# Cutting a streaming encoder step into segments of 128, 256, 256, 256 and 128 + 64 tokens, with row streams that begin and end by themselves

## What is computed

```python
h = layer_norm(x)
P = h @ w_in                          # RWKV-7 columns and differential-attention columns
m = concat(rwkv7(P_rw), diff_attn(P_da)) @ w_out
h = layer_norm(alpha * h + m)
# PEER, for each token: 8 heads, each with 16 rows of two tables of 16384 x 1024
q = h @ wq;  s = q . subkeys          # 2 x 128 scores a head
idx, gate = best 16 of the sums of the best 16 + 16;  softmax
act = gelu(u_tab[idx] . h)            # 128 rows of 4 KB a token
y = layer_norm(alpha * h + sum(gate * act * v_tab[idx]))   # 128 rows more
```

## Time and profile before

| | us |
|---|---|
| median of three runs | 3923.53 |
| lowest and highest run | 3910.43, 3933.09 |
| span of the profiled execution | 4295.2 |
| TensorE busy in it | 2933.3 |
| VectorE busy | 2496.8 |
| GpSimd (POOL) busy | 2395.1 |
| ScalarE busy | 663.3 |
| HBM read | 1315.76 MB, 309 GB/s over the span |

### The profile page before, as it was taken

The page is one execution under the profiler, slowest core; times in us unless marked ns, Lnnn a source line. Parts: engine busy times, 40 slices in busy tenths (PEclk is TensorE's granted clock), DMA queues, the critical chain, the costliest instruction groups (busy, mean ns, idle before and its releaser), DMA issues.

```text
span 4295.2 us, 49152 instructions
## 1 busy us (share of the span) xinstructions
PE 2933.3 (68%) x18591; PEld 1591.0 (37%) x18591; DVE 2496.8 (58%) x5849; ACT 663.3 (15%) x1879; POOL 2395.1 (56%) x2194
## 2 busy tenths in 40 slices
PE   7886376777757777678567777677546565575677
PEld 5666354436324434345034343354112221230111
DVE  3437987665965555578755556569645455583311
ACT  3331122220012212101011222200011111000000
POOL 0001366664556665675665566565566667676765
PEclk9988677898878877789787887788776666687788
DMA  3125688898889987898987898898899889999998
GB/s 117 67 78 205 217 314 308 313 339 348 298 322 337 336 307 274 337 372 323 357 333 277 317 341 293 306 377 310 318 392 355 322 340 356 391 389 347 383 359 315
DMA packets 372965, 1330.61 MB, mean 310 GB/s; under 512 B 40348, under 2 KB 75576, under 8 KB 361592
## 3 DMA queue, kind: packets, MB, share of 16 engines
q0 software_dynamic: 314576, 1145.45, 71.2%
q1 hardware_dynamic: 58152, 182.02, 11.3%
HBM read 1315.76 MB, written 11.29 MB: 309 GB/s over the span
## 4 chain that ended last, share of the span: by engine, by line
PE 19%; issue 15%; DVE 13%; POOL 10%; another core or an unknown queue 8%; DMA 6%; ACT 2%; DVEq 0%; ACTq 0%
PE pacc L1114 7%; POOL ring_v L757 5%; POOL ring_u L757 5%; DMA ring_v<-in_peer_v,idx_t 4%; DVE ring_u L1461 4%; PE pm L1089 3%; PE pm L1075 3%; DMA ring_u<-in_peer_u,idx 2%; PE pm L1306 1%; PE pm L1320 1%; PE pm L1094 1%; DVE arena L1717 1%; DVE arena L1718 1%; DVE arena L1720 1%
## 5 line engine op out<-in xcount | busy, mean ns | idle before, releaser
L757 POOL DMA_INDIRECT ring_u<-in_peer_u,idx x1088 | 1217.3, 1119 | 1106.7 <-DVE gates L1706 402.4
L1461 DVE CUSTOM_DVE_ANT_0 ring_u<-ring_u,h 128x1024 f32<-128x1024 f32 x1088 | 1292.9, 1224 | 528.9 <-DMA ring_u<-in_peer_u,idx 453.2
L757 POOL DMA_INDIRECT ring_v<-in_peer_v,idx_t x1032 | 1116.9, 1082 | 741.1 <-PE pacc L1114 434.3
L1114 PE MATMUL pacc<-ring_v,spread_w 128*32 128x512 f32 x4128 | 1085.2, 763 | 495.3 <-DMA ring_v<-in_peer_v,idx_t 362.1
L1114 PEld LDWEIGHTS pacc<-ring_v,spread_w 128*32 128x32 f32 x4128 | 174.8, 123 | 1131.3 <-DMA ring_v<-in_peer_v,idx_t 725.1
L1075 PE MATMUL pm<-hT,wts 128*128 128x256 f32 (+2 forms) x2656 | 536.7, 359 | 41.9 <-issue 33.3
L1089 PE MATMUL pm<-arena 64*64 64x64 f32 (+1 forms) x6256 | 372.1, 254 | 282.8 <-issue 166.6
L1075 PEld LDWEIGHTS pm<-hT,wts 128*128 128x128 f32 x2656 | 455.7, 204 | 154.5 <-issue 98.5
L1089 PEld LDWEIGHTS pm<-arena 64*64 64x64 f32 x6256 | 292.0, 155 | 445.9 <-issue 278.1
L1075 PE MATMUL pm<-wts,hT 128*128 128x384 f32 (+1 forms) x576 | 199.8, 501 | 6.6 <-DMA wts<-in_sets 6.6
L1075 PE MATMUL pm<-wts,mixT 128*128 128x128 f32 (+1 forms) x1152 | 170.1, 297 | 38.8 <-issue 27.9
(11 more groups left out here) (233 smaller groups left out, 2775.6 us busy)
## 6 DMA issues: line engine op xcount, KB each, us to landing
wts<-in_sets SPq DMA_DIRECT2D x82, 1536.0 KB
ring_u<-in_peer_u,idx POOLq DMA_INDIRECT x1088
ring_v<-in_peer_v,idx_t POOLq DMA_INDIRECT x1032
wts<-in_sets SPq DMA_DIRECT2D x11, 1024.0 KB
arena<-in_subkeys SPq DMA_DIRECT2D x5, 1024.0 KB
arena<-in_x_prompt SPq DMA_DIRECT2D x8, 512.0 KB, 14.0
out<-arena SPq DMA_DIRECT2D x64, 64.0 KB
out<-h POOLq DMA_DIRECT2D x8, 512.0 KB
```

The costliest lines, as they stand in the source:

```text
L757: pool.indirect_dma_start(out=out, out_offset=None, in_=table, in_offset=bass.IndirectOffsetOnAxis(ap=index.bitcast(U32), axis=0)).then_in ...
L1114: x = pe.matmul(pacc[out, c, :], spread_w[:, blocks % 2, quad, place % EIGHTH, :], row[:, c * 512:(c + 1) * 512], start=(place == 0), stop ...
L1461: v.tensor_tensor_reduce(ring_u[:, row, :], ring_u[:, row, :], h1[:, g % 4, :], 1.0, 0.0, ALU.mult, ALU.add, dots[:, slot:slot + 1]).then_ ...
```

## The change

Segments become 128, 256, 256 and 256 prompt tokens, and a last one with 128 prompt tokens (tile 7) and the stream's 64 (tile 8) side by side. Each segment has one pass after its pairs. `rows`, `sample` and so on become lists by tile, and a segment has spans by stream: shift, state and history switch between prompt and stream at the span's edge. The cached keys and values go into the place of prompt keys 512 to 1023 once the prompt tile of that head is done. u and v streams get opens and closes of their own, and a table says which of them lie beside which part of a segment. The mixing of segment 1 carries u of tile 0 in its first 0.60 and half of tile 0's v in the rest. After the mixing three rounds are left: u7 with v6, u8 with v7, v8. The descriptor space of the software DMA is set to 4096 bytes, and the arena grows by 192 numbers.

```diff
-SEGMENTS = [Segment(i, False, i * SEG, SEG) for i in range(SEQ // SEG)] + [Segment(SEQ // SEG, True, 0, DEC)]
+SEGMENTS = [Segment(0, 0, P, 0, 0), Segment(1, P, SEG, 0, 1), Segment(2, P + SEG, SEG, 0, 3), Segment(3, P + 2 * SEG, SEG, 0, 5),
+            Segment(4, P + 3 * SEG, P, 1, 7)]
...
+    def own_keys(self, t):
+        return SEQ if self.sample[t] else self.start + t * P
+    def first_key(self, t):
+        return SEQ - PAST if self.sample[t] else 0
+    def stream(self, c):
+        return 1 if c * CH >= self.spans[0][2] else 0
...
+    return [("project", s, 0), ("norm", s, 0), ("query", s, 0)] + [("topk", s, t) for t in range(s.tiles)]
...
+def u_rows(g):
+    return [("u_open", g, None)] + [("u", g, (q, part)) for q in range(u_pieces(g)) for part in range(2)] + [("u_close", g, None)]
+def v_rows(g, lo=0.0, hi=1.0):
+    n = v_pieces(g)
+    out = [("v", g, (q, c)) for q in range(round(lo * n), round(hi * n)) for c in range(2)]
+    return [("v_open", g, None)] * (lo == 0) + out + [("v_close", g, None)] * (hi == 1)
...
+ROUNDS = {
+    1: [(0.60, u_rows(0), []), (0.40, [], v_rows(0, 0.0, 0.5))],
+    2: [(0.42, u_rows(1), v_rows(0, 0.5, 1.0)), (0.58, u_rows(2), v_rows(1))],
+    3: [(0.50, u_rows(3), v_rows(2)), (0.50, u_rows(4), v_rows(3))],
+    4: [(0.50, u_rows(5), v_rows(4)), (0.50, u_rows(6), v_rows(5))],
+}
...
+    for s in SEGMENTS[1:]:
+        mixes = merged(s)
...
+        for part, us, vs in ROUNDS[s.n]:
...
+            order += spread(mixes[at:end], us, vs)
...
+        order += alternate(u_rows(g) if g < len(TILES) else [], v_rows(g - 1))
...
+                    if s.last:
+                        sp.wait_ge(S["o_read"], attn_tiles(s, j) + 1)
+                        sp.dma_start(keysT[:, SEQ - PAST:SEQ], ins["old_keys"][j]).then_inc(S["hist"], 16)
+                        sp.dma_start(vals[:, (SEQ - PAST) // P:KT], ins["old_values"][j].rearrange("p (b e) -> p b e", e=P)).then_inc(S["hist"], 16)
...
+                            if s.sample[t]:
+                                tl.next(S["hist"], 32)
...
-    nc = bacc.Bacc("TRN2", target_bir_lowering=False, num_devices=1)
+    nc = bacc.Bacc("TRN2", target_bir_lowering=False, num_devices=1, dynamic_dma_scratch_size=4096)
```

More of the change, by code:

```diff
@@ L91, in main_steps @@
         steps += [("rwkv", s, j), ("levels", s, j), ("chunks", s, j)]
-    return steps + [x for part in closing(s) for x in part]
+    return steps + closing(s)
 def closing(s):
[L97 to L104, removed]
+    return [("project", s, 0), ("norm", s, 0), ("query", s, 0)] + [("topk", s, t) for t in range(s.tiles)]
 def maps(s, t):
-    return [(0, 1)] if s.past + t * P + s.rows <= 512 else [(0,), (1,)]
+    return [(0, 1)] if s.keys(t) <= 512 else [(0,), (1,)]
 def stage(name, n, parts):
@@ L132, in merged, with closed @@
             out += [y for y, at in zip(a, places) if at == i]
[L133 to L144, removed]
-            out += stage(kind, n, [("main", kind, s, j)])[0]
-        elif len(s.passes) > 1:
-            out += stage("project", n * 3, [("main", kind, s, j)])[0]
+    return out + closed(s)
+def closed(s):
+    both = stage("project", 1, [("main", "project", s, 0), ("main", "norm", s, 0)])
+    out = both[0] + both[1] + stage("query", 1, [("main", "query", s, 0)])[0]
+    for t in range(s.tiles):
+        out += stage("topk", s.tiles, [("main", "topk", s, t)])[0]
     return out
 def folds(g):
-    return P // TILES[g][0].rows
+    return P // tile_rows(g)
 def u_slots(g):
@@ L1029, in mixing @@
                     elif kind == "query":
-                        n, own = pass_number(s, j) * 2 * PH, columns(s, j)
+                        n, own = s.n * 2 * PH, slice(0, s.width)
                         for c in range(2 * PH):
@@ L1325, in mixing @@
                         tl.next(S["o_ready"])
-                        for t in range(s.tiles):
+                        for t, r in enumerate(s.rows):
                             x = pe.transpose(pm[:, 4, P + t * P:P + t * P + r], qk[0:r, t, 0:P], ident[0:r, 0:r])
@@ L1627, in mixing @@
                         tl.next(S["rms_ready"])
-                        tl.link(v.reciprocal(rms[0:r, 0:s.tiles], rms[0:r, 0:s.tiles]))
-                        for t in range(s.tiles):
+                        for r, of in alike(s):
+                            tl.link(v.reciprocal(rms[0:r, of], rms[0:r, of]))
+                        for t, r in enumerate(s.rows):
                             x = v.tensor_scalar(qk[0:r, t, 0:P], qk[0:r, t, 0:P], rms[0:r, t:t + 1], None, ALU.mult)
```

404 lines of the change are left out of this document (204 added, 200 removed).

## The result

The changed kernel takes 3973.0 us (median of four runs, 3968.6 to 3974.4) beside 3925.4 for the kernel before on the same chip: ratio 1.0128, 95% interval 1.0105 to 1.0151. It is slower by 48 us, where 19 us faster was the forecast, at a chance of 0.42 for faster and 0.38 for slower; the range 3800 to 4015 holds it.

The account below looks back on a forecast made before the run. Stretches with few gathers were taken as paced by VectorE's and TensorE's in-order queues, the rest by each gather's varying price. Six terms summed to 4295 us, the old span; two scalings averaged 3904, range 3800 to 4015.

Parts of the forecast that it names:

- The head: Segment 0 of 128 tokens, before any gather: 294 us for 405.0, 111 us less (bounds 266 and 344).
- Term 3: Segment 2 with 448 gathers: 815 us (780 to 870), between 833 by the 1.57 us line and about 800 by pairs.
- Term 2: Segment 1, 256 tokens with 128 u and 64 v gathers: 588 us (bounds 490 and 660).
- From the profile to the median: Whole kernel: converts the 4295.2 us profiled span to the 3923.5 us median; forecast mean 3904.
- Both scalings: Whole kernel: even scaling by 0.9135 gives 3923; scaling only what follows the first 882 us by 0.88 gives 3885.
- Terms 4 and 5: Segment 3 with 512 gathers, 930 us; merged segment 4 with 512, 907 us (850 to 950), including four 3 us waits.
- The tail: After the last top-k: 512 gathers instead of 256, with a new u7 and v6 round; 761 us for 432.2.
- Early rows don't get cheaper: Slower rival: segment 1's pairs stay at 101 to 107 us, segment 2's at 144; 4015 us, chance 0.22.
- The gathers run at the best slice's pace: Faster rival where less mixing is beside gathers: 1.32 us each, tail 50 us shorter; about 3790, chance 0.20.
- I am wrong if tail gathers take 1.3: Sign against the forecast, which put tail gathers at 1.38 to 1.47 us each.
- The head hardly shrinks: Rival for segment 0: 344 us instead of 294, as pairs are steps more than columns; about 3965, chance 0.09.
- the descriptor space is short: Rival: POOL waits for descriptor room, gathers cost 1.92 us each behind the head; 4480 or 4090, chance 0.04.

Follow-up runs that it names:

- the two kernels on chip 11: Changed kernel with the stream split off as sixth segment, 4416.95 us; changed kernel with 16 of 128 rows in u4 and v3 gathers, ratio 1.0073.

## Why the prediction was wrong

Against the differences between the two profiles on chip 1, each of the six terms had the right sign:

| term | predicted | measured |
|---|---|---|
| 1 head | −111 | −108.5 |
| 2 rest of segment 0, segment 1 | −215 | −189.6 |
| 3 segment 2 | −90 | −50.1 |
| 4 segment 3 | −16 | −12.3 |
| 5 segment 4 | +103 | +109.0 |
| 6 tail | +329 | +310.0 |
| sum | 0 | +58.5 |

*The head* came out nearly as read: first gather at 302.5 us (294), the last three 128-token pairs 43.3, 42.3 and 40.9 us (39.5):

```profile
302.53 1.12 POOL L788 DMA_INDIRECT ring_u<-in_peer_u,idx  x1 [299.62 <-DVE gates L1747]
```

*The steps that failed are terms 2 and 3, mis-sized by 65 us.* Term 3 took 1.57 us for a gather that leaves a full segment, from 200.9 us for 128 gathers between two stages of the earlier trace rows, and by the pairs went below that line: 90 us for 46 gathers is 1.96 each. The same two stages on chip 1 give (796.7 − 648.5) / 128 = 1.16, which for 46 gathers is 53, near the 50.1; so of the 40 us that term 3 is off, 19 are the first profile's excess in the slope, 18 the step below the line, and 3 remain. And part of the slope is mixing: without rows segment 2 is 55.5 us longer than segment 1 (566.1 − 510.6), with 80 matmuls more, since its tokens see more earlier keys. "The mixing work is alike" was false; net of it 92.7 us are left for 128 gathers, 0.72 each, less than half of what was taken. Segment 2 of the changed kernel says so too: 55 gathers fewer (439 for 494) gave 14.0 us net of mixing, and the other 36.1 of the 50.1 are a segment that starts 128 tokens earlier (530.0 for 566.1 without rows).

Term 2 predicted 588 and got 557.2, which looks favourable; but the stage it is held against was 746.8, not 802.6: the new stage was put 31 us too long, and the old one, taken from the first profile, is 56 too long. Pairs with 34 u rows took 78.8 and 81.5 us (88):

```profile
414.20:493.00 78.80, 61.87 (x599) 46.25 (x598) 66.49 (x132) 25.97 (x77) 47.15 (x34) 0.85 0.76 274
493.00:574.50 81.50, 63.80 (x599) 47.67 (x598) 66.62 (x132) 26.04 (x77) 46.41 (x34) 0.83 0.75 265
```

*From the profile to the median* hid this. Both scalings took a sum of zero for granted. The second one had the right idea, that the excess lies beside the gathers, but it held everything before 1207.6 us for paced by instructions and equal in the profile and in the runs. Of that stretch 704.2 us were 648.5 on chip 1: segment 1's gathers carried 56 us of the excess, and the gain was credited with them. Where an unprofiled median and a profiled span differ by 9.5%, the heads of two profiles would have told at once that mixing is not what differs (405.0 and 410.7 us); with one profile at hand, the price of a removed gather should have been scaled down with the excess in segment 1 too.

*Terms 4 and 5* hold. Without rows the merged last segment is 549.7 us for 346.8, 203 more, of which 109 show, as the gathers beside it take their time anyway. The wait for the old keys and values was put at four times 3 us; TensorE's waits in the changed kernel (line, what it waited for, us in total, times, longest) have 8.2 each, 32.7 together and 21 more than the sum had, inside the bounds of nothing to 14.0:

```profile
PE pm L1344 <- DMA arena<-in_old_values: 32.7, 4, 8.9
```

*The tail* has the predicted shape, 708.1 us for 761: the new round 346.5 (365), u8 with v7 253.7 (265.6), at 1.35 and 1.32 us a gather instead of 1.43 and 1.38, and 12 us of segment 4's round left instead of 25. As a difference it is 19 us less than predicted (310.0 for 329), which made up for a part of the 65.

*The rivals.* "Early rows don't get cheaper" has the sign of the result and not its mechanism: it needed pairs of 33 rows over 98 us, and pairs of 34 took 79 to 82; the 204 gathers of segment 1 cost 54.7 us, 0.27 each, where 396 cost 154.0, 0.39 each, before. "The gathers run at the best slice's pace" had its condition met, 1.32 to 1.35 us in the tail, and 3790 did not follow, because the kernel before runs at that pace as well; its 397 GB/s was compared with a before from the slower profile. Its 3790 was also missummed: 4137 by the two scalings is 3779 and 3743. "I am wrong if tail gathers take 1.3" was all but met, and it came from the profile and not from the change: the kernel before has 1.32 on chip 1. "The head hardly shrinks" and "the descriptor space is short" are out by measurement. What happened was none of them: the forecast's mechanism in every stage, with 0.90 us given back for a gather and 1.34 paid in the tail. The price p of a gather beside mixing from which the change would pay follows: 45 + 231 x p against 310, p = 1.15 us. That the result stayed inside the range is the width of the range and no merit of the sum.

## What to carry to other kernels

Price what a move takes away by the difference that remains when the rest is taken out, not by the slope between two stages that differ in other work as well; a run of each kernel without the streams gives it. Work that is moved from beside other work to a stretch where it stands alone pays its full price (1.34 us a gather here) and gives back only its share (0.90), so here an earlier start would have paid only without lengthening the part that nothing hides. And compare a profile's span with the unprofiled median first: where they differ as here, by 9.5%, the profile may be that of another chip or of a disturbed execution, and differences that come out of its row-bound stages must be scaled before they are summed. The waits that end in "issue" are the quickest sign of it: 459 us on TensorE in the one profile, 4 in the other.

## What the runs showed of the hardware

- *One chip of four was slower where there are rows, and not without them.* The kernel before takes 3916 to 3926 us on three chips and 4335 on a fourth; without rows it takes 2508.3 and 2511.3. In the tail a gather of 512 KB takes 1.48 us on chip 11 (379.2 / 256, at 359 GB/s) and 1.35 on the others (393 GB/s). The Trainium skill, "HBM Reference", section "Specifications (TRN2)", gives some 358 GB/s to a core whose neighbour streams too, and more to a core that streams alone. These two numbers fit that, but another tail round on chip 11 moved 370 GB/s, and whether a neighbour was at work no run here shows. Nor is it the main part: a round with an eighth of the bytes took no less there, and in the first profile the packets of the gathers took 3% more. Most of the excess goes with TensorE waits of up to 20 us for which the profile names nobody: 459 us in the first profile, 366 and 433 in the two kernels on chip 11, and 4 in both kernels profiled again on chips 1 and 3. Whether it was the chip or something beside it on that chip stays open.
- *Gathers of the tail have a second floor just under the first.* With full rows 1.35 us, with an eighth of the bytes 1.20, of which GpSimd's issue is 0.90 busy and 0.30 between.
- *TensorE's granted clock was lower in the round with narrow matmuls, and the mixing's matmuls took longer for it.* TensorE is busy 235.7 instead of 315.6 us and the clock of the stretch is 0.69 instead of 0.88, between the two levels of 1.2 and 2.4 GHz; the stretch is only 5 us shorter. The v matmuls' busy time falls from 142.5 to 33.0 us, 109.5 less, and the mixing's, which are the same, rises from 173.1 to 202.7. So 30 us of busy time were given back, and had the clock stayed, TensorE's share could have come out larger than 5 us. How much larger isn't shown.
